# A three-layer transformer on one core: the first attention computed in head pairs, feature-major, with its probabilities divided before the transposes

## The reference, cut to what matters

```python
def sliding_window_sink_attention(h, w_in, sinks, w_out):   # 16 query heads, 4 key/value heads, head size 64
    q, k, v = split_qkv(h, w_in)
    s = einsum(q, k) * 64 ** -0.5 - slope * dist             # own block of 128 keys and the one before
    s = where(0 <= dist < 128, s, -inf)
    m = maximum(max(s), sink)
    p = exp(s - m)
    denom = sum(p) + exp(sink - m)
    o = einsum(p / denom, v)
    return o @ w_out
```

## Time and profile before

| | us |
|---|---|
| median of three runs (lowest, highest) | 889.74 (888.76, 890.2) |
| the profiled execution | 888.97 |
| its span in the trace | 887.2 |
| TensorE busy in the span | 869.1 (98%) |
| VectorE busy | 538.0 (61%) |
| ScalarE busy | 435.1 (49%) |
| granted TensorE clock, mean of the span | 0.996 |

### The profile page before, as it was taken

The page is one execution under the profiler, slowest core; times in us unless marked ns, Lnnn a source line. Parts: engine busy times, 40 slices in busy tenths (PEclk is TensorE's granted clock), DMA queues, the critical chain, the costliest instruction groups (busy, mean ns, idle before and its releaser), DMA issues.

```text
span 887.2 us, 14279 instructions
## 1 busy us (share of the span) xinstructions
PE 869.1 (98%) x5832; PEld 784.6 (88%) x5832; DVE 538.0 (61%) x586; ACT 435.1 (49%) x595; POOL 45.9 (5%) x109
## 2 busy tenths in 40 slices
PE   8999999999999998999999999999999999999997
PEld 7987899999999997888999999989867999999996
DVE  5866554444456759878675555567676775555553
ACT  6566444433434676743654444436465374444431
POOL 1200100000000200320000000003000000000000
PEclk9999999999999999999999999999999999999998
DMA  9823155555456374336675555444601575555511
GB/s 293 302 96 124 42 190 191 179 192 195 157 189 224 97 244 142 141 96 218 198 239 190 189 189 189 136 130 122 216 32 50 191 240 192 188 188 187 190 44 47
DMA packets 98441, 147.68 MB, mean 166 GB/s; under 512 B 4042, under 2 KB 81938, under 8 KB 98402
## 3 DMA queue, kind: packets, MB, share of 16 engines
q1 hardware_dynamic: 97234, 143.11, 49.1%
q0 software_dynamic: 1120, 4.00, 1.5%
q10 hardware_dynamic: 48, 0.02, 0.0%
HBM read 146.05 MB, written 1.05 MB: 166 GB/s over the span
## 4 chain that ended last, share of the span: by engine, by line
PE 91%; DVE 3%; DMA 2%; ACT 1%; POOL 1%; issue 1%; SPq 0%; ACTq 0%; DVEq 0%; POOLq 0%
PE bank L1893 27%; PE bank L1894 27%; PE bank L1895 27%; DMA w_raw<-in_swa_w_in 2%; PE bank L1967 1%; PE bank L2531 1%; PE bank L2554 1%; PE bank L2516 1%; PE bank L2510 1%; PE bank L2095 1%; PE bank L2107 1%; PE bank L2094 1%; DMA x_norm<-arena 1%; DVE w_lo L1189 1%; PE bank L2284 0%
## 5 line engine op out<-in xcount | busy, mean ns | idle before, releaser
L1189 DVE TENSOR_TENSOR w_lo<-w_raw,w_hi 128x2048 fp32r<-128x2048 f32 (+3 forms) x129 | 289.4, 2251 | 151.8 <-ACT w_hi L676 151.6
L1893 PE MATMUL bank<-xT_hi,w_hi 128*128 128x256 f32 x1068 | 304.6, 285 | 4.5 <-DVE w_lo L1189 4.4
L1895 PE MATMUL bank<-xT_hi,w_lo 128*128 128x256 f32 x1068 | 302.8, 284 | 0.0
L1894 PE MATMUL bank<-xT_lo,w_hi 128*128 128x256 f32 x1068 | 302.8, 283 | 0.0
L676 ACT ACTIVATE w_hi<-w_raw 128x2048 fp32r<-128x2048 f32 (+3 forms) x129 | 241.2, 1877 | 91.6 <-PE bank L1895 83.1
L1893 PEld LDWEIGHTS bank<-xT_hi,w_hi 128*128 128x128 f32 x1068 | 204.7, 192 | 9.3 <-DVE w_lo L1189 4.8
L1894 PEld LDWEIGHTS bank<-xT_lo,w_hi 128*128 128x128 f32 x1068 | 204.7, 192 | 1.9 <-issue 0.2
L1895 PEld LDWEIGHTS bank<-xT_hi,w_lo 128*128 128x128 f32 x1068 | 204.6, 192 | 0.2
L1893 PE MATMUL bank<-w_hi,ff_hi 128*128 128x512 f32 x344 | 134.6, 391 | 0.0
L1894 PE MATMUL bank<-w_lo,ff_hi 128*128 128x512 f32 x344 | 134.3, 390 | 0.0
L1895 PE MATMUL bank<-w_hi,ff_lo 128*128 128x512 f32 x344 | 133.9, 389 | 0.0
(11 more groups left out here) (274 smaller groups left out, 799.3 us busy)
## 6 DMA issues: line engine op xcount, KB each, us to landing
w_raw<-in_ffn_w SPq DMA_DIRECT2D x64, 1024.0 KB, 5.3
w_raw<-in_ffn_w_gate_up SPq DMA_DIRECT2D x22, 1024.0 KB, 5.1
w_raw<-in_ab_w_in SPq DMA_DIRECT2D x12, 1024.0 KB, 5.9
w_raw<-in_ffn_w_down SPq DMA_DIRECT2D x11, 1024.0 KB, 4.8
w_raw<-in_swa_w_in SPq DMA_DIRECT2D x5, 1024.0 KB, 11.0
w_raw<-in_swa_w_out SPq DMA_DIRECT2D x4, 1024.0 KB, 7.4
w_raw<-in_ab_w_out SPq DMA_DIRECT2D x4, 1024.0 KB, 4.9
w_raw<-in_c_w_out SPq DMA_DIRECT2D x4, 1024.0 KB, 5.1
```

Of the source, the lines that this page charges most:

```text
L1189: dve.tensor_tensor(view(w_lo, ch), view(w_raw, ch), view(w_hi, ch).bitcast(F32), ALU.subtract).then_inc(S["lo_done"], 1)
L1893: pe.matmul(out, sh, mh, start=first, stop=False)
L1894: pe.matmul(out, sh, ml, start=False, stop=False)
L1895: return pe.matmul(out, sl, mh, start=False, stop=last)
```

## The change

- `swa_s` holds three groups instead of two. GpSimd writes the sink columns of all four groups early, the last of them once group 0's probabilities are done. Its load of the next gain follows behind that.
- `swa_scores` does a pair of heads per call: the two 128-column matmuls on the two array halves, then the two 256-column ones. `swa_bias` follows per pair; the maxima are a function of their own.
- `swa_normalised` is new: for each pair of heads VectorE makes the reciprocals of the sums, once for each of the three 128-column blocks, and multiplies the 768 probabilities of a partition by them, in place, before the transposes.
- The transposes use bank 3 for every second step. `swa_values` now has the values stationary (64 columns) and the probabilities moving: four matmuls of 256 columns and four of 128, the two heads of a pair on the two column halves. The output is feature-major, so that `swa_output` and TensorE's `swa_operand` go away.
- The pairs of scores of groups 0 and 1 stand between and behind the halves of the query chunks, and the third query chunk's halves have transposes and scores between them. The output projection is issued in its 16 parts, in a new order. Tile 0's parts of the last chunk come before the last parts of tile 1.
- VectorE's and ScalarE's orders are rewritten to match. The low part of chunk 11 moves into `enter`, behind the first residual, and `enter`'s early chunks move ahead of its first normalisation.

```diff
-        swa_s = take(P, 2, 4, SWA_COLS + 2)
+        swa_s = take(P, 3, 4, SWA_COLS + 2)
...
-        SWA_PT_BANK = ((2, 2, 2), (2, 2, 2), (2, 2, 2), (2, 0, 1))
+        SWA_PT_BANK = ((2, 3, 2), (2, 3, 2), (2, 3, 2), (2, 0, 1))
...
+            pool.wait_ge(S["sinks_loaded"], 16)
+            for g in range(4):
+                if g == 3:
+                    pool.wait_ge(S["swa_probs"], 8)
+                pool.tensor_copy(swa_s[:, g % 3, :, 0:SWA_COLS + 2:SWA_COLS + 1],
+                                 sinks[:, 4 * g:4 * g + 4].unsqueeze(2).broadcast_to([P, 4, 2])).then_inc(S["swa_sinks_ready"], 1)
             pool.wait_ge(S["gain_loaded"], 16)
             load_gain(2)
...
+            high_upto(o[1].index + 1)
+            swa_probabilities(0, 0)
+            swa_probabilities(0, 1)
+            swa_transposed(0, 0)
+            swa_probabilities(1, 0)
+            swa_transposed(0, 1)
+            swa_transposed(0, 2)
+            swa_probabilities(1, 1)
+            swa_operand(0)
+            swa_transposed(1, 0)
+            high_upto(o[2].index + 1)
...
             def enter(use, n, early, then):
 
                 add_residual(n, 0)
+                low_upto(early)
                 normalise(n, 0, x_norm)
...
+            def swa_normalised(g, half):
+
+                h = 4 * g + 2 * half
+                dve.wait_ge(S["swa_probs"], 8 * g + 4 * half + 4)
+                dve.reciprocal(swa_rden[:, h:h + 2, 0:2], swa_sum[:, :, h:h + 2].rearrange("p t h -> p h t"))
+                step(dve.reciprocal(swa_rden[:, h:h + 2, 2:3], swa_sum[:, 1, h:h + 2].unsqueeze(2)))
+                p = swa_s[:, g % 3, 2 * half:2 * half + 2, 1:1 + SWA_COLS].rearrange("p j (b k) -> p j b k", b=3)
+                dve.tensor_tensor(p, p, swa_rden[:, h:h + 2, :].unsqueeze(3).broadcast_to([P, 2, 3, P]),
+                                  ALU.mult).then_inc(S["swa_normed"], 1)
...
+            swa_bias(0, 0)
             queries(1)
+            swa_bias(0, 1)
+            swa_maxima(0)
+            low_upto(c[1].index + 1 + SLOTS)
+            swa_bias(1, 0)
+            swa_normalised(0, 0)
+            swa_normalised(0, 1)
+            swa_bias(1, 1)
...
+            queries(3)
+            swa_normalised(1, 1)
+            swa_operand(0)
+            swa_bias(3, 0)
+            swa_maxima(2)
+            low_upto(o[1].index + 1)
+            swa_normalised(2, 0)
+            swa_bias(3, 1)
+            swa_operand(1)
+            swa_maxima(3)
+            swa_normalised(2, 1)
+            swa_normalised(3, 0)
+            swa_normalised(3, 1)
+            low_upto(o[2].index + 1)
+            swa_operand(2)
+            low_upto(o[3].index + 1)
+            swa_operand(3)
             low_upto(o[0].index + 1 + SLOTS)
...
-            enter(1, 1, 0, c[3].index + 1)
+            enter(1, 1, c[1].index + 1, c[3].index + 1)
...
+                for qs, ks, cs in ((slice(0, P), slice(0, P), slice(0, P)), (slice(P, SEQ), slice(0, SEQ), slice(P, SWA_COLS))):
+                    for e in range(2):
+                        at = slice(64 * e, 64 * e + 64)
+                        last = pe.matmul(bank[e][:, cs], swa_qT[at, n, qs], swa_kT[at, g, ks], start=True, stop=True)
+                last.then_inc(S["swa_scores"], 1)
...
+                for m in range(2):
+                    for part in range(2):
+                        for e in range(2):
+                            j = 2 * m + e
+                            out = bank[3][64 * e:64 * e + 64, m * SEQ:(m + 1) * SEQ]
+                            if part == 0:
+                                pe.matmul(out, v[0], pt[:, 3 * j:3 * j + 2, :].rearrange("p a b -> p (a b)"), start=True, stop=False)
+                            else:
+                                last = pe.matmul(out[:, P:SEQ], v[1], pt[:, 3 * j + 2, :], start=False, stop=True)
                 last.then_inc(S["swa_o_psum"], 1)
...
+            swa_queries(1, lambda: swa_scores(0, 0))
+            swa_scores(0, 1)
+            swa_queries(2, lambda: swa_scores(1, 0))
+            swa_scores(1, 1)
+            swa_transposes(0, 0)
+            swa_queries(3, turns_and_scores)
+            swa_scores(2, 1)
             swa_values(0)
+            swa_transposes(1, 0)
+            swa_scores(3, 0)
+            swa_transposes(1, 1)
+            swa_transposes(1, 2)
+            out_part(0, 0, 0)
+            out_part(0, 0, 1)
+            swa_scores(3, 1)
             swa_values(1)
...
+            out_part(2, 0, 1)
+            out_part(2, 1, 0)
+            out_part(3, 0, 0)
+            out_part(3, 0, 1)
+            out_part(2, 1, 1)
+            out_part(3, 1, 0)
+            out_part(3, 1, 1, norm=1)
```

More of the change, by code:

```diff
@@ L781, in swa_probabilities, with swa_transposed @@
                                        accum_out=swa_sum[:, t, h:h + 1]).then_inc(S["swa_probs"], 1)
[L783 to L789, removed]
+            def swa_transposed(g, u):
+                act.wait_ge(S["swa_pt_psum"], 3 * g + u + 1)
+                if u == 0 and g >= 2:
+                    act.wait_ge(S["swa_o_psum"], g - 1)
+                act.activation(swa_pT[:, g % 2, 4 * u:4 * u + 4, :].rearrange("p a b -> p (a b)"),
+                               bank[SWA_PT_BANK[g][u]][:], ACT.Copy).then_inc(S["swa_pt_ready"], 1)
@@ L1358, in _ @@
             dve.wait_ge(S["wsT_psum"], 1)
-            dve.tensor_copy(wsT[:], bank[1][:].rearrange("p (a b) -> p a b", a=BG)).then_inc(S["wsT_ready"], 1)
-            low_upto(c[1].index + 1 + SLOTS)
+            dve.tensor_copy(wsT[:], bank[3][:].rearrange("p (a b) -> p a b", a=BG)).then_inc(S["wsT_ready"], 1)
+            low_upto(c[0].index + 1 + SLOTS)
             dve.wait_ge(S["dist_step"], 3)
-            dve.wait_ge(S["sinks_loaded"], 16)
-            def swa_bias(g):
-                hs = slice(4 * g, 4 * g + 4)
[L1366 to L1379, removed]
@@ L1380, in swa_bias, with swa_maxima @@
+            def swa_maxima(g):
+                hs = slice(4 * g, 4 * g + 4)
                 dve.wait_ge(S["swa_biased"], 4 * g + 4)
+                dve.wait_ge(S["swa_sinks_ready"], g + 1)
                 for t, (a, b) in enumerate(SWA_PARTS):
-                    last = dve.tensor_reduce(swa_mx[:, t, hs], swa_s[:, g % 2, :, a:b], axis=AX, op=ALU.max)
+                    last = dve.tensor_reduce(swa_mx[:, t, hs], swa_s[:, g % 3, :, a:b], axis=AX, op=ALU.max)
                 step(last)
                 dve.tensor_scalar(swa_nm[:, :, hs], swa_mx[:, :, hs], -1.0, None, ALU.mult).then_inc(S["swa_nmax"], 1)
[L1386 to L1396, removed]
@@ L2098, in swa_transposes @@
             def swa_transposes(g, u):
                 n = 3 * g + u
-                if u == 0:
-                    pe.wait_ge(S["swa_probs"], 8 * (g + 1))
-                if n >= 1 and SWA_PT_BANK[g][u] == 2:
-                    pe.wait_ge(S["swa_pt_ready"], n)
-                for b in range(4):
-                    j, part = (4 * u + b) // 3, (4 * u + b) % 3
-                    last = pe.transpose(bank[SWA_PT_BANK[g][u]][:, b * P:(b + 1) * P],
-                                        swa_s[:, g % 2, j, 1 + part * P:1 + (part + 1) * P], ident[:])
@@ new lines, in swa_transposes @@
+                if b == 2 and n:
+                    pe.wait_ge(S["swa_pt_ready"], n - (u == 2))
+                if b == 3:
+                    if g == 0:
+                        pe.wait_ge(S["wsT_ready"], 1)
+                    else:
+                        pe.wait_ge(S["swa_ol_ready"], g)
+                if b < 2:
+                    pe.wait_ge(S["swa_biased"], NQH)
+                for i in range(4):
+                    j, part = (4 * u + i) // 3, (4 * u + i) % 3
+                    last = pe.transpose(bank[b][:, i * P:(i + 1) * P], swa_s[:, g % 3, j, 1 + part * P:1 + (part + 1) * P], ident[:])
```

185 lines of the change are left out of this document (83 added, 102 removed).

## The result

The changed kernel takes 879.35 us (median of four runs, 878.18 to 880.98), the old one beside it 889.74 (888.76 to 890.2): ratio 0.9888, 95% interval 0.9876 to 0.9900. It is faster by 10.4 us, or 1.1% by the ratio; 879.4 was forecast. The profiled execution took 878.9, its span is 877.2 and its mean granted clock 0.994 (before 0.996). That the total fits to 0.1 is luck in part, as the last paragraph on the prediction shows.

The account below looks back on a forecast made before the run. TensorE, busy 98%, was taken as the bound. Terms -6.2 - 4.1 - 2.0 + 0.9 - 0.4 (old waits) + 0.5 + 1.2 = -10.1 took 888.97 to 879.0; forecast 879.4 us, range 876.0 to 884.5.

Parts of the forecast that it names:

- Scores: Score matmuls on TensorE: eight pairs at 0.87 us, 7.0 in all for 13.1 before, saving 6.2 (4.6 to 6.7).
- Values: Value matmuls on TensorE: 1.7 us per group, 6.8 in all for 10.9 before, saving 4.1 (2.9 to 4.9).
- Transposes of the outputs: TensorE's four output blocks per group, 0.5 us each, go away, saving 2.0 (1.6 to 2.4).
- More changes of form: TensorE switching between projections, transposes, scores and values: nine more changes at about 0.1 us, costing 0.9 (0.5 to 1.5).
- the twelve steps on the probabilities stay: TensorE's transposes of the probabilities: twelve steps remain, with no saving counted.
- The wait before transposes (1,1): TensorE waits for VectorE to read bank 3 for group 0, until 57.8 with cover ending at 57.3: 0.5 us more.
- Entry: Before the feed-forward layer: 3.4 us from VectorE's residual, covered by two projection parts (2.8); 1.2 more with second half's wait.
- the walk: Following three engines' queues in order, second query chunk to feed-forward layer: ends at 93.2 for 103.1 us, -9.9.
- VectorE in part: Rival: VectorE partly sets the pace; normalisations at 1.6 us lose 1.3, at 2.2 lose 4.9; 882 to 885, 16%.
- slower: Rival: VectorE's normalisation bounds the kernel, breaking even at 2.85 us each; at 3.0 the time is 890.5; 6%.
- No overlap: Rival: array halves don't overlap; pairs of scores cost 1.7 us, values 2.7, time stays at 889; 5%.
- After the stretch: From the feed-forward layer (103.11 us) on, work is the same and TensorE-bound; longer later stages would show the prediction wrong.

Follow-up runs that it names:

- e2: Changed kernel with both heads of a score pair on the same array half, odd heads' scores left out: 884.99 us, ratio 0.9944 to the old kernel.
- e3: Changed kernel with both heads' values in one column half, head after head, odd heads' outputs left out: 883.39 us, ratio 0.9932 to the old kernel.
- e10: Changed kernel without the normalising multiplies, reciprocals kept: 879.43 us, ratio 0.9887 to the old kernel.
- e5: Changed kernel with chunk 11's low part made ahead of the first residual: 877.64 us, ratio 0.9871 to the old kernel.
- e6: Changed kernel with chunk 10's low part ahead of the last operand half and chunk 11's behind it: 877.11 us, ratio 0.9868 to the old kernel.
- e4: Changed kernel with each normalising multiply made twice: 885.46 us, ratio 0.9952 to the old kernel.
- e9: Old kernel with each pair's four score matmuls together at the second head's place, order otherwise old: 890.19 us, ratio 1.0021 to the old kernel.
- e1: Changed kernel run again unchanged: 878.91 us, ratio 0.9881 to the old kernel.
- e11: Changed kernel run a third time unchanged: 879.38 us, ratio 0.9888 to the old kernel.
- e12: Same kernel as e6, run once more: 877.11 us, ratio 0.9864 to the old kernel.
- e7: Changed kernel with all of tile 0's output projection before both of tile 1's parts of chunk 8: 877.07 us, ratio 0.9862 to the old kernel.
- e8: Changed kernel with the edits of e6 and e7 together: 877.21 us, ratio 0.9864 to the old kernel.

## Why the prediction held, and where it did not

**Scores: right.** 0.86 per pair for 0.87, and e2 shows that it is the overlap that makes it. The sixteen heads before held 0.2 more than the 13.1 and the old waits. **Values: too small.** The step "0.5 by columns and 1.0 if they cost like long ones. I take 0.7" failed: the four short ones cost 0.44, so by columns. The term is -4.8, not -4.1; the new form alone would give -5.1, but the old one was 10.69 and not 10.9, since three groups cost less than the 2.72 of the first. **Transposes of the outputs:** 1.8 for 2.0. For scores the prediction had leaned on columns, for values halfway; one rule for both would have served.

**More changes of form: in its range for what it priced, with a term left out.** +0.9 was forecast. The projections cost 0.4 more and the entry's transposes 0.2 more. But "the twelve steps on the probabilities stay" failed: they stay in number and cost 1.0 less, since steps behind a projection or side by side are cheaper than those between scores in the earlier trace rows (0.44 for 0.59). The net is -0.4 where +0.9 stood. The Trainium skill (TensorEngine Tiling, Key Properties) says that changing the tiling mode drains TensorE. The first long pair of a group's values costs 0.15 more than the second (0.58 for 0.43), and no run here tells a drain in that from the start of any other form.

**The wait before transposes (1,1): right** in place and nearly in size, 0.65 for 0.5. e2, e3 and e10 each take it away or nearly, by a slower TensorE or a faster VectorE.

**Entry: place right, size wrong.** +1.2 was forecast, 2.0 measured. The step that failed is "Chunk 11's low part goes behind the residual and ends 0.2 after the inverse root is there". It assumed that the inverse root is not touched by what VectorE does meanwhile. The low part holds GpSimd's sum from 0.30 to 1.51, and e5 and e6 show it: with the low part elsewhere the sum takes 0.30. e6's wait of 0.8 is what the walk should have found with GpSimd free, so the forecast's 1.2 was 0.4 too much for the rest and had nothing for this. The trace of before had the same event, which I did not look for:

```profile
20.03 2.29 DVE L1189 TENSOR_TENSOR w_lo<-w_raw,w_hi 128x2048 fp32r<-128x2048 f32 x1 [2.60 <-ACT w_hi L676]
```
```profile
21.32 1.17 POOL L555 TENSOR_SCALAR mean_sq<-ssq 128x1 f32<-128x1 f32 x1 [7.75 <-ACT x_norm L708]
```

The sum began inside a low part there too, which ended at 22.32. The Trainium skill (SBUF — State Buffer, Who interferes with whom) says that a VectorE instruction with two inputs in SBUF contends with a GpSimd instruction that reads SBUF. The traces agree: in both kernels the sum ended 0.17 behind the low part.

**VectorE in part, slower: not reached.** A normalisation takes 1.14, and e10 finds nearly all multiplies hidden. ("Eight are 9.8" should have been 9.6 by its own 1.2; VectorE is busy for 52.5 us of the stretch, where 54 was forecast.) e4 lengthens each to 2.13 and the waits grow by 4.9, the walk's number, so the order of queues was read rightly. The break-even at 2.85 was not run. The Trainium skill (TensorEngine Tiling, PSUM Bottleneck) says that packing speeds up TensorE and not the emptying of PSUM. e9's waits agree: 4.7 of the 5.7 us are for instructions that read a bank (L1401, L1375, L786).

**No overlap: refuted** by e2 and e3: without it a pair costs 1.50 and a group's values 2.74.

**After the stretch: 2.0 off, mostly by the clock.** The prediction named "the later stages take longer than before" as a sign of being wrong, and in the first profile they did. "After 103.11 the work is the same" holds; its time in one profile does not, and e9 shows old code there at 785.6 where the profile of before has 784.1. Over all profiles with the changed kernel's stages it lies between 785.1 and 786.2. With one profile of the old kernel and e9, a part of some tenths of a us due to the change can't be excluded. Also outside what was named: the feed-forward layer starts at 91.14, not at 93 to 94.

**The total: luck in part.** The 2.0 cancels against the 1.2 by which the stretch beat the forecast and the 0.8 of the start. And the forecast of 879.4 lies 0.2 to 0.4 below what the prediction's sum and walk give from the median (889.74 less 10.1 and 9.9: 879.6 and 879.8). So the hit to 0.1 is no proof of the sum; the terms above show which parts of it hold.

## What to carry to other kernels

Before a reordering puts a long two-input VectorE instruction beside a small GpSimd one, look whether the GpSimd one is on a path to TensorE; a 0.3 us sum can cost 1.5. The packed matmul forms here were worth their columns, down to 128, but e9 shows that this becomes time only if VectorE and ScalarE keep up: price the pair and walk the three queues. And of one profile's clock nothing should be taken as the kernel's: compare the same stage in several profiles before its difference is explained.

## What the runs showed of the hardware

- A one-column GpSimd instruction took 1.51 instead of 0.30 beside a low part of VectorE (2.29), and 1.17 instead of 0.30 at the start of the old kernel.
- Behind the wait of 2.04 on TensorE the granted clock stayed at 1.00 in some profiles (after, e1, e3, e11) and fell to 0.50 in others (e2, e4, e10), with the same length of wait; in e2 this cost 1.6. What decides between them isn't settled.
- fp32 matmuls of 256 columns cost 0.43 alone and 0.22 each in pairs on two halves, those of 128 columns 0.22 and 0.11. The old values' matmuls of 64 columns, with the full array, cost 0.22 as well, as much as 128 columns, and 0.43 in e9 where the clock was 0.50.
- The versions with a shorter entry, e6 (and e12), e7 and e8, take 877.07 to 877.21 and can't be told apart. e6 is 12.5 and 11.8 less than the old kernel beside it, and 1.8 to 2.3 less than the changed kernel in its three measurements (878.91, 879.35, 879.38). Its stretch is only 1.2 shorter; behind the stretch its two profiles take 785.1 and 785.3, for 785.5 to 786.2 in the changed kernel's three, and why isn't shown.
